# Hybrid encoder kernel: the 64-row sample is projected in chunk 0 and worked off inside the last chunk

## The reference, cut to what matters

```python
h = _rmsnorm(x, norm_g)
u = jnp.einsum('btd,de->bte', h, w_in)              # 1024 -> 11 groups of 256
a_b, a_c, a_x, a_g, b_v, b_a, b_g, c_u, c_g, x_q, x_g = jnp.split(u, N_SPLITS, axis=-1)
# A: a_b * conv3(a_c * a_x) * silu(a_g)      B: layernorm(conv31(glu)) -> swish, * silu(b_g)
# C: trailing means of c_u, 64x64 mix, * silu(c_g)      X: attention into 256 memory rows, * silu(x_g)
y = jnp.concatenate([y_a, y_b, y_c, y_x], axis=-1)
return x + jnp.einsum('bte,ed->btd', y, w_out), new_a, new_b, new_p     # then a final rmsnorm
```

## Time and profile before

| | |
|---|---|
| median of 3 runs | 1483.63 us (1483.12 to 1484.98) |
| the profiled execution, its own time | 1483.44 us |
| its span in the trace | 1481.7 us |
| TensorE busy | 1431.8 us, 97% |
| DVE, ACT, POOL busy | 1178.6, 563.4, 217.9 us |
| one chunk of the loop on TensorE | 85.2 us (14 chunks from 153.84 to 1346.69 us) |
| last chunk and sample, first to last matmul | 1346.69 to 1473.04 us |

### The profile page before, as it was taken

The page is one execution under the profiler, slowest core; times in us unless marked ns, Lnnn a source line. Parts: engine busy times, 40 slices in busy tenths (PEclk is TensorE's granted clock), DMA queues, the critical chain, the costliest instruction groups (busy, mean ns, idle before and its releaser), DMA issues.

```text
span 1481.7 us, 32647 instructions
## 1 busy us (share of the span) xinstructions
PE 1431.8 (97%) x11758; PEld 1226.0 (83%) x11758; DVE 1178.6 (80%) x3088; ACT 563.4 (38%) x1238; POOL 217.9 (15%) x180
## 2 busy tenths in 40 slices
PE   5978999999999999999999999999999999999996
PEld 4757888888888888888888888888888888888884
DVE  6997795969789595968869596987959697896965
ACT  6774332433333343423423243333324333332323
POOL 0161110111111011111110111111101111110110
PEclk9989999999999999999999999999999999999998
DMA  9986546455644635565463545555464556446374
GB/s 268 260 300 226 186 115 227 155 184 198 226 173 130 248 120 207 178 219 191 158 246 93 216 170 201 198 195 202 113 235 147 184 198 227 177 136 236 121 245 164
DMA packets 128386, 284.16 MB, mean 192 GB/s; under 512 B 12393, under 2 KB 69405, under 8 KB 128349
## 3 DMA queue, kind: packets, MB, share of 16 engines
q1 hardware_dynamic: 128349, 283.68, 55.7%
HBM read 225.60 MB, written 58.03 MB: 191 GB/s over the span
## 4 chain that ended last, share of the span: by engine, by line
PE 90%; DVE 4%; DMA 2%; issue 1%; ACT 1%; POOL 0%; SPq 0%; ACTq 0%; DVEq 0%
PE u L529 21%; PE u L530 20%; PE u L531 20%; PE sps L529 5%; PE sps L531 4%; PE sps L530 4%; PE qps L529 4%; PE qps L531 4%; PE qps L530 4%; PE ops L610 2%; DMA ring<-wo_split 1%; PE sps L741 1%; DVE z L1392 1%; DVE w_hl L1374 1%; DVE prow L1416 0%
## 5 line engine op out<-in xcount | busy, mean ns | idle before, releaser
L529 PE MATMUL u<-h_hi,w_hl 128*128 128x256 f16 (+1 forms) x2992 | 789.1, 269 | 12.4 <-DVE w_hl L1374 10.2
L530 PE MATMUL u<-h_lo,w_hl 128*128 128x256 f16 (+1 forms) x2992 | 788.1, 269 | 0.0
L531 PE MATMUL u<-h_hi,w_hl 128*128 128x256 f16 (+1 forms) x2992 | 787.9, 269 | 0.0
L1392 DVE SCALAR_TENSOR_TENSOR z<-glu,cst,z 128x256 f32<-128x256 f32 (+1 forms) x1020 | 424.1, 486 | 0.5
L529 PEld LDWEIGHTS u<-h_hi,w_hl 128*128 128x128 f16 x2992 | 293.0, 98 | 58.0 <-issue 12.0
L531 PEld LDWEIGHTS u<-h_hi,w_hl 128*128 128x128 f16 x2992 | 293.0, 98 | 32.9
L530 PEld LDWEIGHTS u<-h_lo,w_hl 128*128 128x128 f16 x2992 | 293.0, 98 | 32.7 <-issue 0.7
L894 ACT ACTIVATE gate<-u,inv 128x256 f32<-128x256 f32 (+1 forms) x204 | 82.7, 456 | 122.1 <-PE u L531 121.9
L1838 POOL TENSOR_TENSOR sa<-cu 128x540 f32<-128x540 f32 (+1 forms) x17 | 30.6, 1802 | 562.8 <-ACT cu L894 499.1
L529 PE MATMUL sps<-ring,y_hi 128*128 128x512 f32 (+1 forms) x262 | 104.1, 397 | 0.1
L529 PE MATMUL qps<-ring,y_hi 128*128 128x512 f32 x258 | 102.6, 398 | 1.4 <-DMA ring<-wo_split 1.4
(11 more groups left out here) (226 smaller groups left out, 1851.3 us busy)
## 6 DMA issues: line engine op xcount, KB each, us to landing
ring<-wo_split SPq DMA_DIRECT2D x256, 512.0 KB, 7.7
ob<-in_x_prompt SPq DMA_DIRECT2D x34, 512.0 KB, 4.1
probs_turned<-probs SPq DMA_DIRECT2D x130, 128.0 KB, 2.4
pt<-probs_turned SPq DMA_DIRECT2D x32, 512.0 KB, 3.5
out<-ob SPq DMA_DIRECT2D x32, 512.0 KB, 3.5
rows_turned<-rows SPq DMA_DIRECT2D x114, 128.0 KB, 2.4
w_hl<-in_w_in SPq DMA_DIRECT2D x20, 512.0 KB, 7.3
wo_split<-ring SPq DMA_DIRECT2D x16, 512.0 KB, 4.9
```

The source lines that it names most:

```text
L529: nc.tensor.matmul(out, a_hi, b_hi, start=first, stop=False)
L530: nc.tensor.matmul(out, a_hi, b_lo, start=False, stop=False)
L531: return nc.tensor.matmul(out, a_lo, b_hi, start=False, stop=last)
L1392: ins = nc.vector.scalar_tensor_tensor(z[:, c, 0:n], glu[:, c, k:k + n], w, z[:, c, 0:n], ALU.mult, ALU.add)
```

## The change

The sample is taken out of the tail in two halves.

In chunk 0 its rows are loaded (64 x 1024), squared and scaled on ACT, multiplied by the gain on POOL, turned by 8 transposes on TensorE, and split on ACT and DVE into `hs`. The three reciprocal roots that are due there (two tiles of memory rows and the sample) become one chain of three columns, `memory_rms`. Its eleven projections, `sample_project(g)`, stand between chunk 0's last groups. Their raw sums are copied out of PSUM by three ACT instructions and stored to memory, 0.7 MB in all.

In the last chunk the sums come back, into `w_hl` regions of groups that the last chunk has already projected: `b_a`'s for the sums and the states, `x_q`'s for keys and values, and so on (the tuple `S` names the sample's own buffers). Everything else of the sample then runs beside the last chunk's own steps, and its 16 out pieces come at the end. The last chunk no longer prepares a next tile of rows.

```diff
 def first_chunk():                                   # TensorE
     project(0, N, "x_q")
+    sample_transposes()
     memory_product(0)
 ...
     scores(0, N, 1)
+    for g in range(4):
+        sample_project(g)
     project(0, N, "b_g")
     weight_sums(10)
+    for g in range(4, 7):
+        sample_project(g)
     project(0, N, "c_g")
     attend(0, N, 0)
     mix(0, N)
+    for g in range(7, 9):
+        sample_project(g)
     project(0, N, "x_g")
     z_rows(0, N)
     attend(0, N, 1)
+    for g in range(9, 11):
+        sample_project(g)
     out_begin(0, N)
 ...
+def sample_project(g):
+    ...
+    bank = qps[:, k % 2, :]
+    for c in range(CT):
+        f, o = CT * g + c, (CT * (g - RAW_BANKS[k][0]) + c) * SAMPLE
+        for kt in range(KT):
+            ins = three(bank[:, o:o + SAMPLE], w_hi[:, f, kt, :], w_lo[:, f, kt, :], hs[:, 0, kt, :], hs[:, 1, kt, :],
+                        kt == 0, kt == KT - 1)
 ...
 def states_in():
-    pe.wait_ge(kt_l.sem, 2)
+    pe.wait_ge(r_ok.sem, r_ok.at(LAST, 0))
     pe.wait_ge(st_in.sem, 48)
 ...
 def last_chunks():                                   # TensorE
+    project(LAST, N, "b_a")
+    project(LAST, N, "b_v")
+    project(LAST, N, "x_q")
+    states_in()
+    project(LAST, N, "c_u")
+    scores(LAST, N, 0)
+    project(LAST, N, "a_c")
+    keys_t(1)
+    value_sum(1)
+    project(LAST, N, "a_x")
 ...
+    out_pieces(LAST, N, Z_AT, 10)
+    mix(i, n)
+    for p in range(PAIRS):
+        attend(i, n, p)
+    out_pieces(LAST, N, 10, PIECES)
+    states_out(0, N)
+    z_rows(i, n)
+    sample_pieces(0, 6)
+    states_out(1, SAMPLE)
+    sample_pieces(6, 10)
+    z_back(i, n)
+    sample_pieces(10, PIECES)
 ...
 def last_chunks(x_here, y_here):                     # SP
     residual(LAST, N, x_here)
     for q in range(RING):
         ring_load(LAST, q)
-    for p in range(PAIRS):
-        probs_across(LAST, p, N)
 ...
+    for k in range(3):
+        sp.wait_ge(raw_out[k].sem, 16)
+    raw_returns(0)
     sp.dma_start(st_rows[0:HB, 0:GW], state_conv_b[0, 0]).then_inc(st_in.sem, 16)
     sp.dma_start(st_rows[0:HP, GW:2 * GW], state_pool[0, 0]).then_inc(st_in.sem, 16)
     sp.dma_start(st_rows[0:HA, 2 * GW:3 * GW], state_conv_a[0, 0]).then_inc(st_in.sem, 16)
+    sp.wait_ge(u_ready.sem, slot(LAST, "x_q")[0])
 ...
+    probs_across(LAST, 0, N)
+    raw_returns(1)
+    sp.dma_start(xs, x_sample[0]).then_inc(res_s.sem, 16)
+    probs_across(LAST, 1, N)
+    probs_across(CHUNKS, 0, SAMPLE)
+    sp.wait_ge(u_ready.sem, slot(LAST, "x_g")[0])
+    for b in range(RING):
+        sp.dma_start(late[b].bitcast(F32), wo_split[b]).then_inc(wo_late.sem, 16)
+    for q in range(RING, PIECES):
         ring_load(LAST, q)
 ...
 def last_chunks():                                   # DVE
+    histories(LAST)
+    normalise(LAST - 1, N)
+    glu_out(LAST, N)
+    taps_free(LAST)
+    taps(LAST, N, 0, 6)
+    q_low(LAST, N)
+    taps(LAST, N, 6, 10)
+    histories_in()
+    glu_out(i, n)
+    taps(LAST, N, 10, 11)
+    softmax_max(LAST, N, 0)
 ...
```

More of the change, by code:

```diff
@@ L103, in encoder_program @@
         with nc.sbuf_tensor("w_late", [P, 2, NG, 2, HALF], F32R) as w_late:
-            late = [w_late[:, b % 2, b // 2] for b in range(RING)]
+            late = [w_late[:, b % 2, 7 + b // 2] for b in range(RING)]
+        with nc.sbuf_tensor("sample_r", [P, 2, NG, 2 * HALF], F32R) as sample_r:
+            pass
+        with nc.sbuf_tensor("sample_f", [P, 2, NG, 2 * HALF], F32) as sample_f:
+            pass
         w_hl = sb("w_hl", [P, 2, FT, KT, P], F16)
@@ L184, in encoder_program, with work @@
+        def work(i):
+            return S if type(i) is int and i == CHUNKS else C
         U = [ctx.enter_context(nc.psum_tensor(f"u{b}", [P, HALF], F32)) for b in range(3)]
@@ L282, in emptied @@
                 name, j = FIRST[n], 0
+            elif type(i) is int and i == CHUNKS:
+                name, j = {"mix": ("x_g", LAST), "zf": ("zf", LAST), "zb": ("zf", CHUNKS)}[name]
             else:
@@ L840, in last_chunks @@
+                project(LAST, N, "a_b")
+                for p in range(PAIRS):
+                    scores(i, n, p)
+                project(LAST, N, "a_g")
+                attend(LAST, N, 0)
+                mix(LAST, N)
+                project(LAST, N, "b_g")
+                project(LAST, N, "c_g")
+                attend(LAST, N, 1)
+                project(LAST, N, "x_g")
+                z_rows(LAST, N)
                 out_begin(LAST, N)
-                out_pieces(LAST, N, 0, 4)
-                value_sum(1)
@@ L863, in last_chunks @@
-                project(CHUNKS, SAMPLE, "b_g")
-                project(CHUNKS, SAMPLE, "c_g")
-                project(CHUNKS, SAMPLE, "x_g")
-                z_rows(CHUNKS, SAMPLE)
-                for p in range(PAIRS):
-                    attend(CHUNKS, SAMPLE, p)
-                out_begin(CHUNKS, SAMPLE)
-                pe.wait_ge(va_ok.sem, va_ok.at(CHUNKS, 1))
+                z_rows(i, n)
+                sample_pieces(0, 6)
                 states_out(1, SAMPLE)
-                out_pieces(CHUNKS, SAMPLE, 0, Z_AT)
@@ L1047, in cu_out @@
                 act.wait_ge(hist_ok.sem, hist_ok.at(i, 3))
[L1048 removed]
+                if needed(d_ok.at(i, 0)) and work(i) is C:
                     act.wait_ge(d_ok.sem, d_ok.at(i, 0))
[L1050 removed]
+                scaled_out(i, n, "c_u", work(i).cu[:, :, HP:HP + n], ACT.Copy, cu_ok)
             def d_high(i, n):
```

616 lines of the change are left out of this document (409 added, 207 removed).

## The result

The changed kernel takes 1493.38 us (median of 5 runs, 1491.45 to 1493.93) against 1483.98 for the kernel before in the same session: a ratio of 1.0059, interval 1.0045 to 1.0073. On the 1483.63 us that the prediction started from, this is 1492.4. The forecast was 1488: the direction is right, the size is twice the predicted one (8.8 us for 4.4), and the time lies outside the forecast's own 1484 to 1491 and at the upper end of its range for 8 in 10, 1479 to 1493. All ratios are of undisturbed executions; two of the experiments' executions, 1652 and 5164 us long, are left out. The profiled execution took 1493.54, its span is 1491.7.

The account below looks back on a forecast made before the run. TensorE, 97% busy, was taken as the bound. Span 1481.7 - 24.0 (end) + 7.1 (chunk 0) + 15.1 (states) + 2.2 (clock) + 1.7 + 2.0 + 0.6 (small waits) = 1486.4, with 1.7 outside: 1488 us; 8-in-10 range 1479 to 1493.

Parts of the forecast that it names:

- What bounds the kernel: Whole kernel: TensorE, 97% busy, bounds it; waits 13.7 us in chunk 0, 6.2 at the end, none in the loop.
- Removed from the end: Last chunk and sample: eleven projections (16.5 us), their lower-clock loss (1.3) and four waits (6.2) go, 24.0 us in all.
- The wait for the states: Last chunk, before the states' six transposes: TensorE waits for state loads queued behind eight ring loads, +15.1 us, bounds 7.1 and 16.
- The clock in `c_u`: Last chunk, behind the wait for the states: TensorE's clock is at the lower level in this projection, +2.2 us.
- `value_sum(1)`: Last chunk: this step waits for ACT's squares, which stand behind the exponentials and the sample's `c_u`, +1.7 us.
- The sample's `z`: End of the kernel: it is back 0.6 us after the sample's out piece 11, a new wait of +0.6 us.
- The ring load of out piece 8: Last chunk: this load stands behind eight `w_late` loads and lands after TensorE wants it, +2.0 us, at least 1.
- DVE is not bound: Last chunk: DVE, given the sample's work, still has 5 us of slack before `z_rows`, so counted 0.
- The second rival's range: Last chunk: DVE becomes the bound, with a 3 to 7 us wait of `z_rows` or `mix`: 1491 to 1495 us, 16%.
- Chunk 0, the eleven projections and what the gaps fill: Chunk 0: projections add 16.5 us, filled gaps return 7.5, avoided lower clock 4.3, new lower clock adds 1.5: +6.2 us.
- the clock behind `c_g`: Chunk 0, after this projection: 3.8 us of idling lowers TensorE's clock, costing 1.5 us, bounds 0 and 3.4.
- Chunk 0, the rest: Chunk 0: eight transposes add 0.9 us; ACT's and POOL's sample work costed at nothing, at most some 4 us if uncovered.

Follow-up runs that it names:

- the last experiment: Best reordered kernel (1468.61 us), with GpSimd's gain product of the sample's rows held until DVE has made tile 5's low part: 1468.11 us, ratio 0.9879.

## Why the prediction was right in direction and too small in size

- **What bounds the kernel**: right: nearly all that was found was a wait of TensorE, its lower clock or its own work. Three readings of the kernel before were off and changed nothing: its loop does wait, 1.13 and 0.22 us for ring loads; chunk 0 has a sixth wait, of 1.62 us at 147.86, which the changed kernel has too; and of the two small stores behind the eight loads the first landed at 1455.60, 0.6 us before the last load.
- **Removed from the end, 24.0 us**: the sum of the last stretch bears it out: -24.0 plus what was measured there (14.5 + 1.4 + 1.4 + 4.7 + 1.1 = 23.1) is -0.9, and the stretch shrank by 0.6.
- **The wait for the states, +15.1**: 14.5. The place, the releaser and the landing (T = 30.3 for 30.9) were right, and so was the reason: the run with four ring loads in front moved it by 5.7 us, the run with the states first took it away.
- **The clock in `c_u`, +2.2**: 1.4. **`value_sum(1)`, +1.7**: 1.4. **The sample's `z`, +0.6**: 1.1.
- **The ring load of out piece 8, +2.0**: no wait in the changed kernel, 4.3 us once the wait in front of it was taken away (2.6 by the landing in the changed kernel). The mechanism was right, the size too small, and another wait hid it.
- **DVE is not bound, 0**: this is a step that failed, by 4.7 us (2.96 and the clock behind it). The slack that it worked out was there (the run with the states first). But a slack says how much an engine can do in all, not when it turns to the one thing that is waited for: 8.4 us of the sample's steps stand between `ya_out` and `z_stats` of the last chunk. With the norm put first the wait was gone, so the order suffices as its cause; about 3 of the 8.4 us are DVE standing still beside GpSimd, and no run took these alone away. The second rival's range, 1491 to 1495, holds the measured time by luck: no wait of `z_rows` or `mix` came.
- **Chunk 0, the eleven projections and what the gaps fill**: 6.2 forecast, 5.9 in the trace, 6.1 by leaving them out. Inside it the waits left are 5.4 us and the pause 0.6, for 6.2; the clock behind `c_g` costs 2.7 for 1.5 (the mix and two projections take 6.3 us from 122.32 on, at full clock 0.8 + 2.8), within its bounds of 0 and 3.4.
- **Chunk 0, the rest**: "Costed at nothing here: ACT's squares (1.25), scaling (1.0), high part (0.55) ... hidden by ACT's own idling" is the other step that failed. The rest costs 4.3 us where 0.9 was counted. By the starts in the trace: 1.5 before `b_a` (0.5 to 1.5 in the traces of the experiments that load the sample at this place; the load of 0.25 MB, which the prediction put at 0.6 "of the next weights" and then left out), 1.1 before `x_q` (DVE standing still beside GpSimd's product), 0.8 for the transposes, 0.8 before `a_b` (a wait for ACT; that the sample's work on ACT makes it is shown for 0.3 at most). ACT is idle for 62% of the span, but between 22 and 60 us, where the weights of chunk 0 go through it, for 4.8 us of 38. An average over the span was read where the stretch alone counts, and of the bound that the prediction itself gave (at most some 4 us) the lower end was taken. The stretches of ACT in the kernel before show it (length, busy):

```profile
22.00:40.00 18.00, 15.31 (x27) 1.00 0.92 263
40.00:60.00 20.00, 17.87 (x29) 1.00 1.18 299
```

The misses add up: +3.4 in chunk 0 before the projections and -0.3 behind, +2.7 for DVE's order (4.7) less the ring load's 2.0, -1.2 for states, clock, `value_sum` and the sample's `z`, +0.5 in the loop (it takes 1192.3 to 1193.6 us in the experiments, so this is scatter), and 0.2 that no term holds: the 5.3 us by which the span exceeds the forecast.

## What to carry to other kernels

Work that is moved into gaps is paid for by what prepares it, in front of the gaps, as much as by itself: here 4 of 10 us. Before an edit is costed at nothing for an engine's idle time, read that engine's idle time in that stretch, and read also which instruction in its order the bounding engine will want next.
A few small loads behind a queue of large ones wait for all of them. The change lost 15 us to a place on SP's list; with five changes of order, and no work taken away, the same change is 1.2% faster than the kernel before.
When two waits lie one behind the other, removing the first can show nothing: the trace, not the time, says whether the edit worked.

## What the runs showed of the hardware

A DVE instruction whose operands lie in SBUF can stand still while GpSimd works on its own: a scaling of 128 x 1024 took 3.45 us beside a GpSimd product of 2.36, 1.28 alone; in the last chunk two scalings of 64 columns took 2.51 us beside GpSimd's `y_lo` and gate product (2.53 us together, from 1437.64), 0.48 alone. It also goes the other way: a GpSimd product that takes 1.3 us alone took 2.29 when DVE's low part of 1.27 had begun 0.13 us before it. The Trainium skill has this rule in "SBUF — State Buffer", section "SBUF: two separate sides": GpSimd and DVE share one pair of ports, which whichever starts first holds for its whole instruction while the other fully blocks; of DVE's instructions it names those with two inputs in SBUF and those in a mode that uses two ports. The traces agree for instructions with two inputs, both scalings among them; the first taps of the last experiment have one. The prediction did not draw on the rule, and put GpSimd's product at nothing.
